# Hybrid GLA/MLA layer in fp32r on one core: both token halves of an MLP-up tile side by side, and interleaved columns in MLP down

## The reference

```python
D_MODEL, SEQ, D_FF = 1024, 1024, 4096
h = _rmsnorm(x, mlp_norm[l])
x = x + jnp.square(jax.nn.relu(h @ w_up[l])) @ w_down[l]
```

## Time and profile before

| | us |
|---|---|
| median of the runs shown (2) | 1269.46 (1269.12 to 1269.81) |
| the profiled execution, span from first to last instruction | 1269.5 |
| in front of MLP group 0 (input projection, attention, output projection) | 0 to 567.9 |
| the eight MLP groups on PE | 567.9 to 1265.4 |
| busy: PE / PEld / DVE / ACT / POOL | 1239.4 / 1012.9 / 496.8 / 392.9 / 309.3 |

### The profile page before, as it was taken

The page is one execution under the profiler, slowest core; times in us unless marked ns, Lnnn a source line. Parts: engine busy times, 40 slices in busy tenths (PEclk is TensorE's granted clock), DMA queues, the critical chain, the costliest instruction groups (busy, mean ns, idle before and its releaser), DMA issues.

```text
span 1269.5 us, 16050 instructions
## 1 busy us (share of the span) xinstructions
PE 1239.4 (98%) x5970; PEld 1012.9 (80%) x5970; DVE 496.8 (39%) x810; ACT 392.9 (31%) x795; POOL 309.3 (24%) x311
## 2 busy tenths in 40 slices
PE   5999999989999999999999999999999999999998
PEld 5967677868787888888888888888888888888887
DVE  5355966436665642352313222222223122222222
ACT  5344433135555552334212122033032121220310
POOL 2432635001100043413320331133023303311300
PEclk9999999989999999999999999999999999999999
DMA  7322423291000016202210220122022102201102
GB/s 238 89 83 69 130 90 95 58 295 37 26 25 26 26 61 222 67 1 67 68 45 22 67 66 13 53 66 65 1 66 66 50 16 66 66 18 48 33 33 99
DMA packets 52031, 86.75 MB, mean 68 GB/s; under 512 B 5584, under 2 KB 18912, under 8 KB 51984
## 3 DMA queue, kind: packets, MB, share of 16 engines
q1 hardware_dynamic: 50432, 81.22, 20.2%
q10 hardware_dynamic: 1008, 3.67, 0.8%
q0 software_dynamic: 544, 1.24, 0.5%
HBM read 69.33 MB, written 16.78 MB: 68 GB/s over the span
## 4 chain that ended last, share of the span: by engine, by line
PE 91%; DVE 4%; issue 2%; ACT 1%; DMA 1%; POOL 1%; SPq 0%; ACTq 0%; DVEq 0%; POOLq 0%
PE ps L1180 86%; PE ps L1401 2%; PE ps L1195 1%; DVE g_cum L931 1%; PE ps L1253 1%; POOL wi_lo L423 1%; DMA gain<-in_attn_norm_dram 1%; ACT q_stage L555 0%; PE ps L1338 0%; PE ps L1322 0%; DMA raw<-in_w_in_dram 0%; PE ps L1267 0%; DVE rk L860 0%; PE ps L1433 0%; DVE m_qk L905 0%
## 5 line engine op out<-in xcount | busy, mean ns | idle before, releaser
L416 POOL TENSOR_TENSOR w_lo<-raw,w_hi 128x512 fp32r<-128x512 f32 x128 | 166.6, 1330 | 486.3 <-ACT w_hi L555 485.4
L1180 PE MATMUL ps<-a_hi,w_hi 128*128 128x512 f32 x512 | 199.3, 389 | 0.0
L1180 PE MATMUL ps<-a_hi,w_lo 128*128 128x512 f32 x512 | 199.2, 389 | 0.0
L1180 PE MATMUL ps<-a_lo,w_hi 128*128 128x512 f32 x512 | 199.2, 389 | 0.0
L1180 PE MATMUL ps<-w_hi,act_hi 128*128 128x512 f32 x512 | 199.2, 389 | 0.0
L1180 PE MATMUL ps<-w_lo,act_hi 128*128 128x512 f32 x512 | 199.2, 389 | 0.0
L1180 PE MATMUL ps<-w_hi,act_lo 128*128 128x512 f32 x512 | 199.2, 389 | 0.0
L555 ACT ACTIVATE w_hi<-raw 128x512 fp32r<-128x512 f32 x144 | 85.2, 626 | 331.7 <-PE ps L1180 249.7
L1172 DVE TENSOR_TENSOR xs<-ps,xs 128x512 f32<-128x512 f32 x128 | 87.4, 692 | 237.6 <-PE ps L1180 237.6
L1163 DVE TENSOR_TENSOR relu<-relu 128x512 f32<-128x512 f32 x64 | 45.1, 705 | 267.2 <-ACT act_hi L815 267.2
L1180 PEld LDWEIGHTS ps<-a_hi,w_hi 128*128 128x128 f32 x512 | 96.1, 188 | 20.1 <-issue 0.2
(11 more groups left out here) (175 smaller groups left out, 1601.5 us busy)
## 6 DMA issues: line engine op xcount, KB each, us to landing
raw<-in_w_up_dram SPq DMA_DIRECT2D x64, 256.0 KB, 3.0
raw<-in_w_down_dram SPq DMA_DIRECT2D x64, 256.0 KB, 3.0
raw<-in_w_in_dram SPq DMA_DIRECT2D x24, 256.0 KB, 3.1
z_gla<-z_stage SPq DMA_DIRECT2D x16, 256.0 KB, 2.1
raw<-in_w_out_dram SPq DMA_DIRECT2D x16, 256.0 KB, 7.2
xs<-in_x_dram SPq DMA_DIRECT2D x8, 512.0 KB, 8.9
x<-in_x_dram ACTq DMA_DIRECT2D x7, 512.0 KB, 4.9
out_dram<-xs SPq DMA_DIRECT2D x7, 512.0 KB, 2.6
```

Of the source, the lines that this page charges most:

```text
L416: pool.tensor_tensor(w_lo[half][:, k, :], raw[:, k % RING, :], w_hi[half][:, k, :].bitcast(F32), ALU.subtract).then_inc(wlo_done, 1)
L1180: return pe.matmul(dst, lhsT, rhs, start=start, stop=stop)
```

## The change

MLP up: the loop over (half, f) is turned round. For each f both token halves are computed together, into two neighbouring banks (2 * (f % 2) + half), and for each k-step and each of the three products the two halves follow each other, with the same stationary operand. ACT and DVE take the tiles in that order (`f, half = divmod(j, 2)`). The waits at the head of group 0 move: the transposes of block 7 and the wait for `alo_done` 32 now stand ahead of the first matmul of the group. The wait for free banks is taken once per pair.

MLP down: for f = 1, 2, 3 output bank and moving operand are both addressed in another order, the same for both, so that the same values reach the same addresses: 256 columns of the first half of the bank and 256 of the second are taken in turn, in runs of 2 (f = 1), 4 (f = 2) and 32 (f = 3). For f = 0 the order is as before. The wait for `actlo_done` follows the new numbering of the tiles.

```diff
@@ ScalarE group, and VectorE group
-                    half, f = divmod(j, FT)
+                    f, half = divmod(j, 2)
@@ TensorE
+            def ordered(tile, f):
+
+                run = (W, 2, 4, 32)[f]
+                return tile if run == W else tile.rearrange("p (a c e) -> p c a e", a=2, e=run)
+
             def group(g, first):
-                for j in range(2 * FT):
-                    half, f = divmod(j, FT)
-                    if first and j == 0:
-
+                for f in range(FT):
+                    if first and f == 0:
                         pe.wait_ge(alo_done, 2 * NB + NB)
-                    if first and j == 1:
                         norm_T(1, NB - 1, xn2[:, (NB - 1) % 2, :])
-                    if first and j == FT:
                         pe.wait_ge(alo_done, 4 * NB)
-                    cols = slice(half * W, (half + 1) * W)
-                    pe.wait_ge(up_bank_free, 2 * FT * g + j + 1)
+                    pe.wait_ge(up_bank_free, 2 * FT * g + 2 * f + 2)
                     for k in range(KT):
-                        if j == 0:
+                        if f == 0:
                             pe.wait_ge(wlo_done, 2 * KT * g + KT * Q_UP + k + 1)
                         wh = w_hi[0][:, k, f * P:(f + 1) * P]
                         wl = w_lo[0][:, k, f * P:(f + 1) * P]
-                        last = split_product(ps[:, j % 4, :], wh, wl, a_hi[:, k, cols], a_lo[:, k, cols],
-                                             k == 0, k == KT - 1)
-                    last.then_inc(up_ready, 1)
+                        for w, a in ((wh, a_hi), (wh, a_lo), (wl, a_hi)):
+                            for half in range(2):
+                                last = mm(ps[:, 2 * (f % 2) + half, :], w, a[:, k, half * W:(half + 1) * W],
+                                          k == 0 and w is wh and a is a_hi, k == KT - 1 and w is wl)
+                                if k == KT - 1 and w is wl:
+                                    last.then_inc(up_ready, 1)
 
                 for quad in range(NB // 2):
                     for f in range(FT):
-                        pe.wait_ge(actlo_done, 2 * FT * g + FT * (quad // 2) + f + 1)
+                        pe.wait_ge(actlo_done, 2 * FT * g + 2 * f + quad // 2 + 1)
...
-                            last = split_product(ps[:, 4 + s, :], act_hi[:, f, blk], act_lo[:, f, blk],
-                                                 w_hi[1][:, kk, :], w_lo[1][:, kk, :], f == 0, f == FT - 1)
+                            last = split_product(ordered(ps[:, 4 + s, :], f), act_hi[:, f, blk], act_lo[:, f, blk],
+                                                 ordered(w_hi[1][:, kk, :], f), ordered(w_lo[1][:, kk, :], f),
+                                                 f == 0, f == FT - 1)
```

## The result

| | before | after |
|---|---|---|
| median, us | 1269.46 | 1337.3 (1337.03 to 1337.56) |
| span of the profiled execution, us | 1269.5 | 1335.3 |
| ratio to before | | 1.0536 (95% interval 1.0505 to 1.0567) |

The change costs 68 us, 5.4%. The forecast was 1276.9 us with a range of 1255 to 1297, so the measured time lies outside it.

The account below looks back on a forecast made before the run. The prediction took TensorE's matmul pace to bound the MLP; 0 (up) + 0 (columns) + 5.7 (seam) + 1.7 (clock) + 0 (waits) = +7.4 us gave 1276.9 us, range 1255 to 1297.

Parts of the forecast that it names:

- What bounds the kernel: MLP: bound by TensorE's pace alone, 226.7 ns for each matmul; no engine, bank or transfer makes it wait.
- the clock: Pause ahead of group 0: TensorE's clock may fall to half behind it; 1.7 us taken, range 0 to 3.4.
- the seam: Ahead of group 0: up tile 0 now also waits for block 7, 6.6 us late, 5.7 us net.
- Same weights, another bank: MLP up: repeating weights for two neighbours and changing bank at each matmul cost 0; possible gain up to 20.6 us.
- Interleaved columns: MLP down, f = 1, 2, 3: 1152 reordered matmuls cost 0; bounds 15.4 us gained to 232 us lost.
- nearest row: For short runs in MLP down: DVE's 682 ns in runs of at most 32 against 690 for 512, speaking for no cost.
- Rival C: MLP down, f = 1: runs of 2 are slow, 201 ns each, 77 us more, 1354 us; chance 0.16.
- Its own point of decision: MLP down: the whole change is over 2% slower once f = 1 matmuls alone lose 47 ns each.
- Rival D: MLP down: every broken order is slow, 201 ns for 1152 matmuls, 232 us more, 1509 us; chance 0.03.
- The waits inside the groups: Within MLP groups: waits between up and down, for banks and for converted weights stay hidden; cost 0.
- Nothing to convert: Whole kernel: profiled span 1269.5 and median 1269.46 agree, so the sum was added without conversion.

Follow-up runs that it names:

- the seam alone: Kernel before with only block 7's transposes and the wait for all low parts moved ahead of up tile 0, tiles in old order: 1279.01 us, ratio 1.0062.
- the whole up part: Changed kernel with all MLP down columns back in natural order, side-by-side up tiles and moved waits kept: 1280.9 us, ratio 1.0077.
- the one-side kernels: Kernel before; MLP down writes PSUM or reads the moving operand in runs of 2, 4 or 32; runs of 2: 226.7 ns written, 338 read.

## Why the prediction was wrong, point by point

**What bounds the kernel** (right). One unbroken piece before and after; nothing but the turns, the clock's part in them included, and the seam moved the time.

**Same weights, another bank** (right, at 0). 699.08 us side by side, 698.94 in the old order, behind the same seam.

**Interleaved columns** (wrong, the step that failed). I took 0 and it was 56.1 us. The bounds were sound: runs of 2 were given at most 201 ns, measured 112. What failed was the choice between them. The "nearest row" was DVE's 682 ns in runs of up to 32, a row of another engine at a lower pace and with runs of at least 64 bytes, and it was given the weight of evidence. It could not speak of runs of 8 bytes. The other reason given, that the number of columns and the addresses stay the same, fell too: 512 columns took 338.5, 251.0 and 236.7 ns by their order alone. The rows that did bear on it were read, and then left as a curiosity: a surplus of 13.4 ns at full clock and none at half. Read with the later runs, natural order was already at the limit of its supply at the full clock, with 226.7 ns at 128 pieces and 216 at 64, so an order that asks more of the supply had nothing to draw on. I had named a collision with the weight load as a possible cause; loads of 137 in place of 188 ns left the turn at 231 ns. Rival C had the right place; its price of 201 ns was nearly twice the 112 measured, and that the whole came within 17 us of its 1354 owes something to runs of 4 and 32, which it held free. Its own point of decision, 47 ns for each matmul of f = 1, was passed by 65.

Of the pages of the Trainium skill that were weighed, the page "PSUM — Partial Sum Buffer", Specifications, says that a non-contiguous pattern in PSUM slows matmuls significantly. No run here agrees, since with PSUM written in runs of 2, 4 and 32 the turn was 226.7 once settled. The page "Advanced Engine Details and Errata" of the Trainium skill, Memory Cachelines, asks for at least two hits on a 16-byte line of SBUF. Two were not enough here: fp32r at the full clock took 338 to 459 ns with two columns at a visit, unless the same two pieces were read over and over (218). The 16 bytes that it names fit the runs of 4 columns, 340 ns late and 250.6 aligned. The prediction wrote that this section asks "only" for two neighbours in PSUM; it also says, as the PSUM page of the Trainium skill does, that any non-contiguous pattern slows matmuls significantly, so the two did not disagree there.

**Rival D** (all broken orders at 201 ns) fell: 24 and 10 ns for runs of 4 and 32.

**The seam** (right). Predicted 5.7 us net; measured 6.7 - 0.9 = 5.8. The order in the chain was as worked out: `norm_x`, block 6's low parts, two parts of transposes, the last low part as what released TensorE.

**The clock** (right in kind, at the upper half of its range). 1.7 us taken, 2.2 measured; the fall lasted 6.8 us, but the first 1.4 us of it lay in the pause.

**The waits inside the groups** (right, at 0). No wait stands between up and down.

So, without the columns, the sum was 7.4 us. By the medians the seam alone measured 8.3 us (0.62%) and the whole up part 10.2 (0.77%), with intervals that overlap.

**"Nothing to convert"** (wrong, without weight). A time is about 1.7 us more than its span; that the median before and the profiled span agreed was chance.

## What to carry to other kernels

A turn that is steadily longer than columns over clock, by 13 of 227 ns here, is a sign, not noise: find out what supplies the stream before changing its order. For a moving operand of 4-byte columns at the full clock, count the 16-byte pieces that it newly visits; keep runs aligned to 16 bytes, at 64 columns or more if two places are read in turn (64 columns cost nothing here, 32 cost 10 ns), and put a permutation on the PSUM side, where runs of 2, 4 and 32 were free. And when a cost has no row, a row of another engine is not a nearest row; keep the middle of the bounds until one of the same engine excludes it.

## What the runs showed of the hardware that I had not expected

- Where new pieces of 16 bytes were read going forward, the turn was close to 1.77 ns for each: 226.7 ns at 128 pieces, 257 at 144, 300 at 170, 438 to 459 at 256. With 64 pieces it took 216 ns, so natural order in fp32r is itself held up by the reading. Short runs took 427 ns at half clock and 328 at full, so their pace is one in time and not in TensorE's steps. The count by 1.77 ns is 4.5 to 6.5 ns too low for a late beginning, for 4 of every 8 columns and for 432 columns.
- Pieces read a moment ago cost nothing: two of them in turn, up to 1024 bytes apart, gave 218 ns. Yet runs of 2 in turn from two halves, where each piece is visited twice with one visit elsewhere between, took 338.5 ns, one and a half times natural, and late runs of 4 took 340. Why they cost this, and why aligned runs of 4 to 32 take 237 to 251 ns with the same 128 pieces, is open.
- Turns after a slower stretch mostly end in the same series (236, 228, 233, 231, then 226.7 for good), in the one-side kernels, with runs of 128 and in the changed kernel behind the half clock alike. Behind runs of 32 natural order had 226.7 at once.
- A bf16 matmul between fp32r ones cost 20 ns net and not a gain; its weight load was not begun early, and its stationary operand had a stride. Which of these is the cause was not separated.
